# Hybrid trunk step on one core: the vector engine prepares the next attention tile before it copies this tile's turned probabilities

## The reference

```
def block_attention(q, k, v):
    ...
        s = jnp.einsum('bqkgd,btkd->bkgqt', q_blk, k, preferred_element_type=jnp.float32) * ATTN_SCALE
        p = jax.nn.softmax(s, axis=-1).astype(v.dtype)
        return jnp.einsum('bkgqt,btkd->bqkgd', p, v)
```

## Time and profile before

| what | value |
|---|---|
| median of 3 runs | 2430.79 us |
| the profiled execution, its own time | 2433.58 us |
| its span, first to last instruction | 2431.6 us |
| mean granted TensorE clock over the span | 0.953 of full speed |
| busy: PE, DVE, ACT, POOL | 2186.2, 1126.1, 830.7, 317.3 us |

### The profile page before, as it was taken

How to read it: one execution, slowest core, us unless ns; L and a number is a source line. 1 busy time by engine, 2 the same in 40 slices (tenths; PEclk the granted TensorE clock), 3 DMA queues, 4 the chain that set the end, 5 groups by cost and what they waited for, 6 DMA issues and landing times. The chain is left out here.

```text
span 2431.6 us, 58582 instructions
## 1 busy us (share of the span) xinstructions
PE 2186.2 (90%) x26179; PEld 1875.3 (77%) x26179; DVE 1126.1 (46%) x2038; ACT 830.7 (34%) x1504; POOL 317.3 (13%) x542
## 2 busy tenths in 40 slices
PE   5999877878999999979996888888887889999999
PEld 3678654557999999954784767777775789999998
DVE  1242465434542343245324777777784364324421
ACT  4252353333221122143223555655653232112211
POOL 1000130001000000200001433434442100000000
PEclk7999998989999999979997999999998899999999
DMA  7211007860222222112100000000000222222221
GB/s 253 80 37 70 1 1 276 304 227 18 87 70 73 85 70 71 52 26 104 70 35 10 4 9 7 9 10 9 9 6 5 104 62 78 70 80 77 70 77 54
DMA packets 160742, 167.74 MB, mean 69 GB/s; under 512 B 13788, under 2 KB 117996, under 8 KB 160364
## 3 DMA queue, kind: packets, MB, share of 16 engines
q1 hardware_dynamic: 160492, 164.00, 20.9%
HBM read 160.44 MB, written 3.54 MB: 67 GB/s over the span
## 5 line engine op out<-in xcount | busy, mean ns | idle before, releaser
L168 PE MATMUL psum<-arena 64*64 64x64 f32 (+6 forms) x17072 | 838.0, 248 | 146.2 <-DVE arena L1952 16.2
L168 PEld LDWEIGHTS psum<-arena 64*64 64x64 f32 (+3 forms) x17072 | 668.9, 146 | 353.2 <-issue 160.7
L168 PE MATMUL psum<-hidden_high,weights_low 128*128 128x320 f32 x1024 | 233.4, 309 | 0.0
L168 PE MATMUL psum<-hidden_high,weights_high 128*128 128x320 f32 x1024 | 233.3, 309 | 0.0
L168 PE MATMUL psum<-hidden_low,weights_high 128*128 128x320 f32 x1024 | 233.2, 309 | 0.0
L638 ACT ACTIVATE weights_high<-weights 128x2048 fp32r<-128x2048 f32 x62 | 118.6, 1913 | 335.3 <-PE psum L168 335.3
L168 PE MATMUL psum<-norm_high,weights_low 128*128 128x320 f32 x992 | 226.6, 310 | 0.0
L168 PE MATMUL psum<-norm_low,weights_high 128*128 128x320 f32 x992 | 226.6, 310 | 0.0
L168 PE MATMUL psum<-norm_high,weights_high 128*128 128x320 f32 x992 | 226.5, 310 | 0.0
L701 DVE SCALAR_TENSOR_TENSOR arena<-psum,ada,arena 128x320 f32<-128x320 f32 (+2 forms) x96 | 36.3, 434 | 314.9 <-PE psum L168 314.9
L168 PEld LDWEIGHTS psum<-hidden_high,weights_high 128*128 128x128 f32 x1024 | 171.3, 188 | 0.0
(11 more groups left out here) (211 smaller groups left out, 2866.2 us busy)
## 6 DMA issues: line engine op xcount, KB each, us to landing
weights<-in_mlp_w SPq DMA_DIRECT2D x64, 1024.0 KB, 5.5
arena<-in_ada_w SPq DMA_DIRECT2D x24, 2048.0 KB, 9.4
arena<-in_ab_w_in SPq DMA_DIRECT2D x6, 2048.0 KB, 7.8
arena<-in_ab_w_out SPq DMA_DIRECT2D x2, 2048.0 KB, 9.2
arena<-in_rwkv_wv SPq DMA_DIRECT2D x2, 2048.0 KB, 7.7
arena<-in_rwkv_wr SPq DMA_DIRECT2D x2, 2048.0 KB, 8.3
arena<-in_rwkv_wk SPq DMA_DIRECT2D x2, 2048.0 KB, 7.6
arena<-in_rwkv_wo SPq DMA_DIRECT2D x2, 2048.0 KB, 10.5
```

What stands on the lines that cost most here:

```text
L168: return nc.tensor.matmul(out, lhsT, rhs, start=start, stop=stop, skip_group_check=shared)
```

## The change

DVE's stream in the attention stage gets another order; no instruction is added or left out, and the streams of the other engines are the same. The inverses of tile 0 now follow its maxima directly. Then, for each tile m: the maxima of tile m+1, the inverse of tile m+1's head 0, the copy of tile m's head 0, the inverse of tile m+1's head 1, the copy of tile m's head 1. The copies' waits are now made once for each head.

```
-            def turned_rows(m):
+            def turned_rows(m, h):
                 k = keys_of(ATT[m][1])
                 dve.wait_ge(S("att_turned"), m + 1)
                 if m >= 2:
                     dve.wait_ge(S("att_values"), m - 1)
-                for h in range(2):
-                    V.tensor_copy(PT[m % 2][:, h, 0:k], turned(h)[:, 0:k]).then_inc(S("att_pt"), 1)
+                V.tensor_copy(PT[m % 2][:, h, 0:k], turned(h)[:, 0:k]).then_inc(S("att_pt"), 1)
+
+            def inverse(m, h):
+                st = att_small(m, h)
+                dve.wait_ge(S("att_exp"), 2 * m + h + 1)
+                V.reciprocal(st[:, 3:4], st[:, 2:3]).then_inc(S("att_inverse"), 1)
 
             row_max(0)
+            for h in range(2):
+                inverse(0, h)
             for m in range(NA):
-                for h in range(2):
-                    st = att_small(m, h)
-                    dve.wait_ge(S("att_exp"), 2 * m + h + 1)
-                    V.reciprocal(st[:, 3:4], st[:, 2:3]).then_inc(S("att_inverse"), 1)
                 if m + 1 < NA:
                     row_max(m + 1)
-                turned_rows(m)
+                for h in range(2):
+                    if m + 1 < NA:
+                        inverse(m + 1, h)
+                    turned_rows(m, h)
```

## The result

The changed kernel takes 2417.43 us (median of 4 runs, 2415.66 to 2420.36) against 2430.34 us of the kernel before (4 runs). The ratio is 0.9946, with a 95% interval of 0.9928 to 0.9965: faster by 12.9 us in these runs. The profiled execution took 2420.36 us, its span is 2418.4 us. The direction was forecast, the size was not: the forecast was 2424.1 us with a range from 2420.5 to 2428.5.

A forecast was written before the change was run, and what follows sets the result against it. The prediction took a ring of waits in the attention stage as the bound. From the median 2430.79 us it took 6.1 for four pairs of heads and 0.6 for half the clock fall: 2424.1 us, range 2420.5 to 2428.5.

The forecast's parts named there:

- The ring before: Attention stage, long tiles: copies, next tile's inverse, GpSimd's scaling, transposes and copies again wait in turn, 5.01 us a step.
- The ring after: Attention stage, long tiles: with the inverse moved, scores, maxima, exponentials and next scores through one set of banks, 4.30 us.
- the short tile: Two steps at each pair of heads' short tile, scores to scores: 3.8 us, then 4.55 with late maxima.
- The unknown costs: Two costs the trace before could not settle: DVE's switches in the attention stage, and clock falls in later stages.
- (a): DVE's switch from copy to inverse and back: nothing to 0.2 us each, taken as 0.07; at most 1.5 in all.
- (b): Stages behind the attention: the clock may fall at other moments, bounded by about 1.5 us either way.
- The clock in the stage: TensorE's clock fall before tile 3's copies would go: 1.3 us in the profiled execution, 0.6 given to the median.
- The small gain: Rival: gain real but under 4.9 us, through costly DVE switches or one more clock fall; 2426.2 us, chance 0.19.
- the collision with GpSimd: Rival: DVE's copies and GpSimd's scaling hold each other up, long step 5.7 us, total 2439 us; chance 0.04.
- an inverse that waits for the exponential: Rival: DVE stands before head 0's inverse with transposes finished, so little changes; 2430.8 us, chance 0.02.

The follow-up runs named there:

- both_first: The changed kernel with both inverses of the next tile ahead of both copies, in place of head by head; median 2420.25 us.
- before_again: The kernel before, unchanged, run and profiled a second time; median 2427.03 us.
- before_3: The kernel before, unchanged, profiled a third time; attention stage 99.9 us, stages behind it 2054.7 us.
- before_4: The kernel before, unchanged, profiled a fourth time; attention stage 98.6 us, stages behind it 2052.6 us.
- before_split: The kernel before with the copies' waits made once for each head, order as it was; mean 2427.9 us, ratio 1.000.
- before_pad10: The kernel before with 10 idle reductions put at the end of DVE's attention stream; mean 2437.5 us.
- the padded ones: The changed kernel with 3, 5, 8 or 10 (10 twice) idle reductions ending DVE's attention stream; means 2418.6, 2420.6, 2425.9, 2423.5 and 2423.8 us.
- head_scores: The changed kernel with TensorE's scores made head by head, each waiting only for its own head's exponential; median 2418.6 us, mean 2417.2.

## Why the prediction was right in kind and wrong in size

*The ring before.* Right. Copies, inverse, scaling, transposes made 5.01 us, and moving the inverse broke it: 5.6 us in both_first, its share of the clock's fall included. GpSimd's wait for the inverse fell from 59.8 to 48.6 us, by 11.2, where I had some 7.

*The ring after.* Right to the hundredth: 4.30 us forecast and measured, scores to scores. At the short tile I had 3.8 and 4.55; the trace has scores at 288.57, 292.29 and 296.83, which is 3.72 and 4.54. One pair of heads takes 21.17 us (copies at 300.33 and 321.50), against 21.25 forecast and 22.77 before: 1.6 us a pair in place of 1.5. The first pair gained 1.8, the fall of the clock apart, and the last 1.7, where I had put them at "a few tenths in both directions". In sum 6.7 us in place of 6.1 without the clock.

*The unknown costs.* (a) The switch from copy to inverse costs 0.07 us (305.74 to 305.81), the value that I took, at the low end. (b), the later stages, stood in the sum with nothing, and there the range failed: see below.

*The clock in the stage: the term that was sized wrong.* I took the fall of the earlier trace rows for an accident of one execution and gave half of its 1.3 us to the median. All six traces with the old order (before, before_again, before_3, before_4, before_split, before_pad10) have one or two falls behind 280 us in the attention stage; of the 12 traces with the new order none has one while TensorE still works on the stage (in four of the padded ones its clock falls while it waits for the padding). So it belongs to the old order, whole: 1.3 us, in two of the six traces twice that. That the shorter pauses are the reason is argued from their place, not shown by an edit of its own. With the falls the stage is 98.6 to 99.9 us in the four traces of the kernel before and 90.5 to 90.6 in the four of the changed one: **8.4 us** on the mean, not the 6.7 that the forecast of the median used.

*The later stages: the term that was put at nothing.* This is the largest part of the miss. I took nothing for it in the sum and bounded it by "about 1.5 either way" from three runs. Taken over all executions, 10.9 less 8.4 is about 2.6 us. The traces' clock record tells how long TensorE stood at its half level behind the attention:

| traces | half level, us | behind the attention, us |
|---|---|---|
| old order, 6 | 180.9 to 200.0, mean 190.8 | 2052.6 to 2059.1, mean 2056.1 |
| new order, with its variants, 12 | 177.5 to 191.1, mean 184.7 | 2049.3 to 2056.7, mean 2052.7 |

6 us less at the half level, of which each can cost half a microsecond where TensorE is the bound (an estimate), is 3.0 us, and the piece is 3.4 us shorter. Over all 18 traces the two go together (correlation 0.72, where 1 is in step and 0 is none). So the 2 to 3 us that remain of the 10.9 go with time at the lower clock in later stages, above all in the HGRN and RWKV stages, where falls of 3.4 to 24 us come at places that change from execution to execution. *Why* the new order leaves fewer of them stays open: the runs speak against the moment of the start and the padding, they leave the finer waits and the place of the instructions undecided, and both groups overlap so far that part of it may be chance.

*The first comparison was also lucky.* 12.9 us in 4 runs against 4 is 10.9 over all, and the three later comparisons have 9.5, 9.5 and 10.2 us (ratios 0.9961, 0.9961 and 0.9958). The luck is in the kernel before: 2430.8 is the mean of its first four runs, 2.1 us above its 104 executions, while the four of the changed kernel have the mean of its 20. It is not what broke the forecast: 2417.7 lies 2.8 us under the range.

*The miss in one sum.* 6.7 forecast, 0.6 more from the ring, 1.0 more from the clock in the stage, about 2.6 from the later stages and 2.0 of luck make the 12.9 measured.

*The rivals.* The small gain did not come, nor the collision with GpSimd, nor an inverse that waits for the exponential: in a long step DVE does not stand in front of L961 at all (only at the short tiles, 8 times, 3.0 us in sum).

## What to carry to other kernels

When several rings of waits share an engine's stream, write each ring's length as a sum of starts in the timeline: the difference between the first and the second is all that cutting the first can give, and here it was right to 0.01 us a step (5.01, then 4.30). List the third as well: the one of 4.26 us was left out, and the forecast of 3.9 to 4.1 for head_scores failed by it. A pause of TensorE that is shortened can give back more than its own length: the falls of the clock in this stage, 1.3 us each, went with the old order. And where single executions spread over 10 us, three runs do not bound the spread, nor what the stages behind an edit will do; the edited stage's own length in the trace repeats closely (90.5 to 90.6 us in four executions) and shows edits that the total hides, like the 3.0 us of head_scores.

## What was not expected of the hardware

Executions of one kernel differ by up to 13.8 us (2422.1 to 2435.8 in 104). In the 18 traces the short falls of TensorE's clock lie at other places each time, while the three longest behind the attention, of 31 to 38 us, start at the same places within 10 us. In two traces of the kernel before, the later stages differ by 6.5 us (2059.1 and 2052.6) with 191.1 and 180.9 us at the half level.

A DVE copy from PSUM to SBUF beside a GpSimd operation on SBUF is not slowed at all: 0.82 and 0.80 us with it, and 0.82 us without (at 292.40, when GpSimd stands idle). And the scores of the two heads, issued head by head, cost TensorE little more than interleaved (1.58 us for the eight, a wait between them included, at 303.42 in head_scores, against 1.35): the rival that expected 2.6 us for them falls.
